# The four plain units of a split-precision feed-forward block: products kept in PSUM banks, high parts made by ScalarE

## What is computed

```python
def swiglu(x, w_gate, w_up, w_down):
    return (jax.nn.silu(x @ w_gate) * (x @ w_up)) @ w_down

x = x + 0.5 * swiglu(rms_norm(x, ffn1_norm[l]), ffn1_w_gate[l], ffn1_w_up[l], ffn1_w_down[l])
x = x + hybrid_mixer(rms_norm(x, mix_norm[l]), ...)
x = x + 0.5 * swiglu(rms_norm(x, ffn2_norm[l]), ffn2_w_gate[l], ffn2_w_up[l], ffn2_w_down[l])
```

## Time and profile before

| | |
|---|---|
| median of 3 runs | 2694.54 us (2693.35 to 2697.31) |
| the profiled execution | 2694.64 us |
| its span in the profile | 2692.9 us |
| mean granted clock of TensorE | 0.991 |
| TensorE busy | 98% |
| VectorE, ScalarE, GpSimd busy | 56%, 46%, 44% |
| DMA | 240.46 MB, mean 89 GB/s |

### The profile page before, as it was taken

One profiled execution on the slowest core, in us unless ns is written; L12 is line 12 of the kernel. 1 busy time (PEld: TensorE's weight loads), 2 busy tenths in 40 slices (PEclk: granted clock), 3 DMA queues, 4 the chain that ended last, 5 costly groups with the idle time before them and its releaser, 6 DMA issues. The chain is left out here.

```text
span 2692.9 us, 41426 instructions
## 1 busy us (share of the span) xinstructions
PE 2626.8 (98%) x15716; PEld 2227.0 (83%) x15716; DVE 1514.6 (56%) x2243; ACT 1251.5 (46%) x2301; POOL 1186.9 (44%) x688
## 2 busy tenths in 40 slices
PE   7899999999999998999999999999999999989999
PEld 6899988766777787898978989887667778888998
DVE  7543574565556368363683535745665653783533
ACT  5354543645534435363453535335555343353543
POOL 3555643321322346565554655432123224464654
PEclk9999999999999999999999999999999999999999
DMA  4223223310211232323222232233012112222322
GB/s 145 94 95 110 91 98 116 111 48 28 71 59 61 85 105 84 110 97 108 95 94 94 97 108 99 92 115 110 32 40 71 60 59 102 94 89 105 110 95 94
DMA packets 38549, 240.46 MB, mean 89 GB/s; under 512 B 4320, under 2 KB 5600, under 8 KB 16352
## 3 DMA queue, kind: packets, MB, share of 16 engines
q1 hardware_dynamic: 36416, 233.85, 25.4%
q10 hardware_dynamic: 1952, 4.12, 0.4%
HBM read 234.81 MB, written 2.10 MB: 88 GB/s over the span
## 5 line engine op out<-in xcount | busy, mean ns | idle before, releaser
L350 POOL TENSOR_TENSOR wlo<-raw,whi 128x1024 fp32r<-128x1024 f32 (+1 forms) x310 | 689.8, 2226 | 1234.9 <-ACT whi L426 804.2
L1619 PE MATMUL bank<-hhi,whi 128*128 128x512 f32 x816 | 340.0, 417 | 16.9 <-DVE hlo L915 10.5
L426 ACT ACTIVATE whi<-raw 128x1024 fp32r<-128x1024 f32 (+1 forms) x198 | 192.7, 974 | 291.3 <-PE bank L1621 165.6
L1725 PE MATMUL bank<-th,slot_u 128*128 128x256 f32 x1152 | 326.4, 283 | 0.3
L1726 PE MATMUL bank<-tl,slot_u 128*128 128x256 f32 x1152 | 326.1, 283 | 0.0
L1621 PE MATMUL bank<-hhi,wlo 128*128 128x512 f32 x816 | 321.7, 394 | 0.0
L1620 PE MATMUL bank<-hlo,whi 128*128 128x512 f32 x816 | 320.8, 393 | 0.0
L1725 PE MATMUL bank<-hhi,slot_u 128*128 128x256 f32 x864 | 249.0, 288 | 31.4 <-DVE bank L1077 31.4
L1619 PE MATMUL bank<-ff,whi 128*128 128x512 f32 x704 | 274.1, 389 | 0.0
L1620 PE MATMUL bank<-ff,whi 128*128 128x512 f32 x704 | 274.1, 389 | 0.0
L1621 PE MATMUL bank<-ff,wlo 128*128 128x512 f32 x704 | 273.9, 389 | 0.0
(11 more groups left out here) (350 smaller groups left out, 6330.5 us busy)
## 6 DMA issues: line engine op xcount, KB each, us to landing
raw<-cb SPq DMA_DIRECT2D x48, 768.0 KB, 4.2
raw<-gu0a SPq DMA_DIRECT2D x16, 1024.0 KB, 4.9
raw<-gu0b SPq DMA_DIRECT2D x16, 1024.0 KB, 4.9
raw<-pM SPq DMA_DIRECT2D x16, 1024.0 KB, 4.9
raw<-cq SPq DMA_DIRECT2D x16, 1024.0 KB, 4.9
raw<-gu1a SPq DMA_DIRECT2D x16, 1024.0 KB, 4.9
raw<-gu1b SPq DMA_DIRECT2D x16, 1024.0 KB, 4.9
raw<-gu0c SPq DMA_DIRECT2D x12, 1024.0 KB, 4.9
```

The lines of the kernel that those rows point to most:

```text
L350: pool.tensor_tensor(wlo[:, s, 0:w], raw[:, j, lo:lo + w], whi[:, s, 0:w].bitcast(f32), ALU.subtract).then_inc(sem["lo_done"], 1)
L426: A(whi[:, s, 0:(wa, wb)[s]], raw[:, u % 2, s * wa:s * wa + (wa, wb)[s]], ACT.Copy).then_inc(sem["hi_done"], 1)
L1619: mm(outp, wh, mhi, start=start and k == 0, stop=False)
L1725: mm(outp, wh, parts[k][0], start=start and k == 0, stop=False, skip_group_check=True)
```

## The change

The up tiles of all four plain units stay in PSUM: `up_p` is now banks 4 and 5 for units 0 and 1 (written there by `late`) and banks 1 and 3 for units 2 and 3. VectorE makes four products in place in these banks, in the order 2, 0, 1, 3. ScalarE copies each from its bank to the high part (`plain_high`), and VectorE subtracts it to the low part (`plain_low`). The casts of line 1021 are gone. The products and subtractions of units 2, 0 and 1 stand where the plain work stood; that of unit 3 is multiplied before line 1069 of the first Strassen unit and subtracted after it. ScalarE's copies of units 2, 0 and 1 stand after the last Silu, and that of unit 3 after the snapshot of product 0. Since the banks are those that the first two Strassen units use, TensorE waits before product 0 of the first for the third Silu, before its product 1 for unit 2's subtraction, and before product 3 of the first and second for those of units 0 and 1. Bank 1 or 3 is declared free (`unit_free`) by the subtraction where it was by the product of line 1003.

```diff
--- before.py
+++ after.py
@@ -23,6 +23,7 @@
 NST = KF - PLAIN
+PLAIN_ORDER = [2, 0, 1, 3]
 EPS = 1e-6
@@ -200,7 +201,6 @@
         gate_p = [within("gate0", 6, [P, S])[:], within("gate1", 7, [P, S])[:], within("gate2", 14, [P, S])[:], within("gate3", 15, [P, S])[:]]
-        up_p = [within("up0", 42, [P, S])[:], within("up1", 43, [P, S])[:], gate_p[2], gate_p[3]]
         fss = [within("fs0", KD, [P, KD, S]), within("fs1", 2 * KF - KD, [P, KD, S])]
@@ -214,6 +214,7 @@
         b6, b7 = bank[6][:], bank[7][:]
+        up_p = [bank[4][:], bank[5][:], bank[1][:], bank[3][:]]
         p1s = [tmp[:, 2 + j, 0:ST] for j in range(2)]
@@ -242,7 +243,7 @@
             "hhi_ready": 3 * KD, "hlo_ready": 3 * KD, "silu_ready": 2 * PLAIN, "uhi_ready": 2 * NST, "ulo_ready": 2 * NST,
-            "plain_mul": 4, "plain_hi": 2 * PLAIN, "plain_lo": 2 * PLAIN,
+            "plain_mul": 2 * PLAIN, "plain_hi": 2 * PLAIN, "plain_lo": 2 * PLAIN,
             "par_ready": 16, "gate_ready": 3 * KD, "y_ready": 3 * KD, "yhi_ready": KD, "ylo_ready": KD,
@@ -509,8 +510,15 @@
                             A(gate_p[c], bank[2 * (c % 2)][:], ACT.Silu).then_inc(sem["silu_ready"], 1)
+                        for c in PLAIN_ORDER[:3]:
+                            plain_high(f // 2, c)
                         if f == 2:
                             act.dma_start(cur[:], t["params"][lay + 1]).then_inc(sem["par_ready"], 16)
+
+                def plain_high(f, c):
+
+                    act.wait_ge(sem["plain_mul"], me.at("plain_mul", f * PLAIN + PLAIN_ORDER.index(c) + 1))
+                    A(uhi[:, c], up_p[c], ACT.Copy).then_inc(sem["plain_hi"], 1)
 
@@ -570,6 +578,8 @@
                         block_snap(p1s[j], bx[j], n, 0)
+                        if p == 0 and e == 0:
+                            plain_high(f, PLAIN - 1)
                         if e:
@@ -997,30 +1007,28 @@
                         block_low(4, m)
-                        for c in range(2, PLAIN):
-                            dve.wait_ge(sem["silu_ready"], me.at("silu_ready", f // 2 * PLAIN + c + 1))
-                            dve.wait_ge(sem["tile_done"], me.at("tile_done", 2 * (n + c + 1)))
-                            dve.tensor_tensor(up_p[c], gate_p[c], bank[2 * (c % 2) + 1][:], ALU.mult).then_inc(sem["unit_free"], 1)
-                            dve.wait_ge(sem["unit_free"], me.at("unit_free", n + c + 1))
-                            dve.sem_inc(sem["held"], 1)
-                            if c == 2:
-                                plain_product(f // 2, 0)
-                                plain_product(f // 2, 1)
-                                for i in range(3):
-                                    plain_split(f // 2, i)
+                        for c in PLAIN_ORDER[:3]:
+                            plain_product(f // 2, c)
+                        for c in PLAIN_ORDER[:3]:
+                            plain_low(f // 2, c)
 
...
                     dve.wait_ge(sem["silu_ready"], me.at("silu_ready", f * PLAIN + c + 1))
-                    dve.tensor_tensor(up_p[c], up_p[c], gate_p[c], ALU.mult).then_inc(sem["plain_mul"], 1)
-
-                def plain_split(f, c):
-
                     if c < 2:
-                        dve.wait_ge(sem["plain_mul"], me.at("plain_mul", 2 * f + c + 1))
-                    dve.tensor_copy(uhi[:, c], up_p[c]).then_inc(sem["plain_hi"], 1)
-                    dve.wait_ge(sem["plain_hi"], me.at("plain_hi", f * PLAIN + c + 1))
+                        dve.wait_ge(sem["unit_free"], me.at("unit_free", FIRST[f"gu{f}a"] + c + 1))
+                    else:
+                        dve.wait_ge(sem["tile_done"], me.at("tile_done", 2 * (FIRST[f"gu{f}a"] + c + 1)))
+                    dve.tensor_tensor(up_p[c], gate_p[c], up_p[c], ALU.mult).then_inc(sem["plain_mul"], 1)
+
+                def plain_low(f, c):
+
+                    m = f * PLAIN + PLAIN_ORDER.index(c) + 1
+                    dve.wait_ge(sem["plain_hi"], me.at("plain_hi", m))
                     dve.tensor_tensor(ulo[:, c], up_p[c], uhi[:, c].bitcast(f32), ALU.subtract).then_inc(sem["plain_lo"], 1)
+                    if c >= 2:
+                        dve.wait_ge(sem["plain_lo"], me.at("plain_lo", m))
+                        dve.sem_inc(sem["unit_free"], 1)
 
@@ -1059,14 +1067,15 @@
                         j, c = u % 2, j0 + e
-                        if p == 0 and end:
-                            dve.wait_ge(sem["plain_lo"], me.at("plain_lo", (f + 1) * PLAIN))
-                            dve.sem_inc(sem["held"], 1)
+                        if p == 0 and e == 0:
+                            plain_product(f, PLAIN - 1)
                         if e:
...
                         dve.tensor_tensor(tmp[:, j, 0:ST], br[j][:, 0:ST], p1s[j], ALU.add).then_inc(sem["st_c"], 1)
+                        if p == 0 and e == 0:
+                            plain_low(f, PLAIN - 1)
                         if e:
@@ -1084,8 +1093,6 @@
                             block_low(2, n + 1)
-                        if p == 0 and e == 0:
-                            plain_split(f, PLAIN - 1)
                     if p == 2:
@@ -1727,13 +1734,17 @@
 
-                    if e < 2:
+                    if first_t:
+                        pe.wait_ge(sem["silu_ready"], me.at("silu_ready", f * PLAIN + 3))
+                    elif e < 2:
                         pe.wait_ge(sem["unit_free"], me.at("unit_free", u - 1))
...
                     pe.wait_ge(sem["st_lo"], me.at("st_lo", 3 * n + 2))
+                    if first_t:
+                        pe.wait_ge(sem["unit_free"], me.at("unit_free", u - 1))
                     product(1, br[j][:, 0:ST], b21).then_inc(sem["st_mm"], 1)
@@ -1743,6 +1754,8 @@
                         pe.wait_ge(sem["t_lo"], me.at("t_lo", 2 * f + 1))
+                    if p == 0 and e < 2:
+                        pe.wait_ge(sem["plain_lo"], me.at("plain_lo", f * PLAIN + 2 + e))
                     product(3, bw[j], t3).then_inc(sem["st_mm"], 1)
...
                     if first_t:
```

## The result

The changed kernel takes 2660.89 us, the median of 4 runs (2658.37 to 2664.45), against 2694.72 before (4 runs): a ratio of 0.9874, with a 95% interval from 0.9857 to 0.9891. That is 33.8 us less. The forecast was 2659.7, range 2655 to 2671. Run again as the base of the experiments it took 2658.64 (2657.79 to 2660.69) beside 2693.39 for the kernel before, a ratio of 0.9869 [0.9854, 0.9884]: 34.75 us less, where 34.8 was the forecast term. That these two agree to 0.05 is luck, since executions of this one kernel lie 3 to 6 us apart.

A forecast was written before the change was run, and what follows sets the result against it. TensorE was 98% busy, held up mainly before product 6 at four places by VectorE's late addition. Of 41.6 us available, 6.2 of pauses and 0.6 of slower first matmuls remain: 2694.5 - 34.8 = 2659.7, range 2655 to 2671.

The forecast's parts named there:

- What bounds it: TensorE's pauses and low clock in the first Strassen unit of each feed-forward block, the four places: 41.6 us available.
- (1) and (2): VectorE loses four casts per place, products 0.70, subtractions 0.68; ScalarE gains four copies of 0.59, and nothing waits.
- (3): TensorE's new wait at product 1 for unit 2's subtraction is met, margin 0.5 at places 2 to 4.
- (4): GpSimd's piece of s4 gates the block sums; pauses before product 6 of 0.5 at place 1, 1.9 at others.
- (5): TensorE's clock does not fall after a 1.9 us pause; bounds 0 and 6.5 us.
- rival B: The clock falls in the 1.9 us pauses, adding 6.5 us: 2666; chance 0.12.
- (6): Raw data for the next unit but one arrives in time behind the pause, margin 0.7 us.
- The sum: 41.6 less 6.2 for pauses and 0.6 for slower first matmuls: 34.8 us gained, giving 2659.7.
- A: GpSimd's pieces beside the plain work stay slow, up to 1.74; gain 27.8, or 2666.7, chance 0.15.
- C: GpSimd's chain is no gate or ends much sooner, so no pause is left: 2653; chance 0.03.
- D: No change: the pause before product 6 has a cause the profile does not name; 2694, chance 0.03.
- E: Slower: VectorE's PSUM products and subtractions each take as long as an SBUF product, 2.19; 2703, chance 0.02.

The follow-up runs named there:

- the version with `s4` first: Changed kernel with GpSimd subtracting the block of s4 before token block 3 instead of after it; 2653.23 us, ratio 0.9850.
- the run of product 1's margin: Changed kernel with the subtraction of unit 2, which product 1 waits for, moved from first to third of three; 2658.00 us, ratio 0.9870.
- the casts on VectorE: Changed kernel with VectorE making the four high parts itself by casts from PSUM, ScalarE none; 2660.44 us, ratio 0.9872.
- the three with a PSUM input: Changed kernel plus three useless VectorE multiplications per place before the block sums, one input in PSUM; 2662.75 us, ratio 0.9882.
- the same with `s4` first: Kernel before the change with only GpSimd's order changed, the block of s4 ahead of token block 3; 2694.63 us, ratio 1.0002.
- the run with three SBUF inputs: Changed kernel plus three useless VectorE multiplications per place before the block sums, both inputs in SBUF; 2678.68 us, ratio 0.9942.

## Why the prediction was right

**What bounds it.** The 41.6 us that could be had were right: the four places lost 41.6 by count, and the version with `s4` first has 41.0 of them.

**(1) and (2), the prices.** VectorE's products 0.69 and subtractions 0.685 on the mean, forecast 0.70 and 0.68; ScalarE's copies 0.60, forecast 0.59. Block 6 slipped as worked out. "Nothing waits" on ScalarE held, but only because VectorE is fast: with the products in SBUF the same queue cost TensorE two pauses a place, which I had not seen as a path.

**(3) Product 1.** No wait; the subtraction of unit 2 ended at 1034.71, 0.8 ahead of where product 1 was due (forecast 0.5, signals included). That a loss there comes out of the pause before product 6 was shown by the run that moved it.

**(4) What is late next.** GpSimd, with 8.54 us for its five pieces (8.5). At places 2 to 4 the pauses are 1.75 to 1.93, forecast 1.9. Place 1 was off: GpSimd's third piece there starts 1.7 before product 0, where it was 2.7 in the profile before, so the pause is 1.4, not 0.5. I took that distance as fixed. It is 2.69 in both traces with the old order on VectorE and ScalarE, and 1.2 to 2.0 in all nine traces of the changed kernel and its variants, so it came with the change; what moved it is not shown. At place 4 it is 1.4 in both traces of the changed kernel and 2.6 in the run of product 1's margin.

**(5) The clock.** This step failed in the profiled execution. I let the nearest row decide (a pause of 1.71 without a fall) and gave rival B 0.12 for a fall at all three places. It fell at two of four, after pauses of 1.83 and 1.75, and not after one of 1.93; each time it cost 1.5 us. Over four profiles with a pause of 1.1 to 1.9 before product 6 at each place (the changed kernel twice, the casts on VectorE, the three with a PSUM input) it fell at 3 of 16; after those of 3.2 us and more, in the kernel before, in the same with `s4` first and in the run with three SBUF inputs, at 12 of 12. The row that I let decide was one draw too: after the same wait near 41.6 us, 1.9 to 2.1 long in the nine traces of the changed kernel and its variants, the clock fell in seven; in the two traces with the old order (1.7 to 1.8, twice in each) it did not. So within 1.1 to 2.1 us neither the length nor one row told whether it falls; what does is open. By the count of 3 in 16 the term should have been about 0.3 us a place, an estimate, and not one of all or nothing. It is also part of the difference between executions: of the 5.0 us between the two profiled executions of the changed kernel, 3.4 lie at the four places, most of it in the two low stretches.

**(6) Behind the pause.** No wait on raw data appeared.

**The sum.** At the four places 7.3 us were left in the base's profile and 10.7 in the one shown, where the sum had 6.8: place 1 took about 1 us more than its 0.5, and the clock 3.1 more in the one shown.

**The rivals.** A is out: GpSimd went back to 1.3. The rule of the Trainium skill in "SBUF — State Buffer", section "Who interferes with whom", is what these runs show: 5.74 against 2.13 for one operand moved. B held in part, at two places of four in one execution and at none in the other. C is out for the changed kernel; its time came with the version with `s4` first, 2653.2 measured where C gave 2653. D is out. E is out. The Trainium skill's advice in "VectorE: DVE Perf Modes", section "Rules for kernel authors", to copy a matmul's output to SBUF before several operations, did not hold beside a busy GpSimd: there a product or subtraction with both inputs in SBUF took about three times as long as one with an input in PSUM, and a cast from SBUF 1.51 against 0.68. Where GpSimd is idle the trace does not speak against it: at 17.0 us of the kernel before a copy of the same size within SBUF took 0.42.

```profile
L930 DVE COPY tmp<-tmp x1: 419/419/419, 17.0 to 17.0; 128x512 f32<-128x512 f32 x1
```

What was not forecast is how the gain divides. I priced the change whole. The runs show 33 us for the banks alone, 12 for ScalarE's copies alone and 34.75 for both. The copies are worth nothing that can be told beside GpSimd's late `s4`, and 5 to 6 us once that is early.

## What to carry to other kernels

Before moving work off an engine, look at where its operands lie: a VectorE operation with two SBUF inputs beside a busy GpSimd was about three times as long as the same with one in PSUM, and slowed GpSimd too (1.75 for 1.29); beside an idle GpSimd it was not longer (0.69). After a chain is cut, find the wait that ends last next, and try reordering that engine: one line moved was worth 5.4 us here, and nothing while the first chain stood. An engine that works in order and is given a copy also inherits the wait for its input, and everything behind it inherits that.

## What the hardware did that was not expected

In this profile the granted clock fell only after TensorE had resumed: 0.8 us after the pause of 1.83 at place 2, where six matmuls ran at 1.00 and the next ones at 0.51, and 1.4 us after the one of 1.75 at place 4. A longer pause of 1.93 in the same execution had no fall. With ScalarE's copies and the products in SBUF, three pauses of 2.40 stand before product 2: at place 4 the granted clock reads 0.50 from 0.6 us after TensorE resumed, at places 2 and 3 it reads 1.00 (from 2374.75, 1044.20 and 1398.80). And three multiplications with SBUF inputs on VectorE differ widely among themselves, from 1.10 to 2.36 us over 12 of them, while the same with a PSUM input are all within 0.686 to 0.689.
